# Weight slots at a pitch of 4160 bytes instead of 4096 in a float32 transformer layer

## What is computed

```python
def reference(x, mem, rel_bias, ln_g, ln_b, ffn_w_gate, ffn_w_up, ffn_w_down, w_in, ...):
    for l in range(DEPTH):
        x = layer_norm(ALPHA * x + 0.5 * swiglu(x, ffn_w_gate[l, 0], ffn_w_up[l, 0], ffn_w_down[l, 0]), ...)
        x = layer_norm(ALPHA * x + hybrid_mixer(x, w_in[l], conv_w[l], ...), ...)
        x = layer_norm(ALPHA * x + memory_attention(x, mem, xq_w[l], xkv_w[l], xo_w[l]), ...)
        x = layer_norm(ALPHA * x + 0.5 * swiglu(x, ffn_w_gate[l, 1], ffn_w_up[l, 1], ffn_w_down[l, 1]), ...)
    return x
```

## Time and profile before

| | before |
|---|---|
| median of three runs | 1128.38 us |
| the profiled execution | 1126.32 us |
| its span | 1124.3 us |
| TensorE busy | 1114.1 us (99%) |
| VectorE busy | 776.9 us (69%) |
| ScalarE busy | 531.9 us (47%) |
| mean granted TensorE clock | 0.999 |

### The profile page before, as it was taken

The page is one execution under the profiler, slowest core; times in us unless marked ns, Lnnn a source line. Parts: engine busy times, 40 slices in busy tenths (PEclk is TensorE's granted clock), DMA queues, the critical chain, the costliest instruction groups (busy, mean ns, idle before and its releaser), DMA issues.

```text
span 1124.3 us, 17750 instructions
## 1 busy us (share of the span) xinstructions
PE 1114.1 (99%) x6752; PEld 992.1 (88%) x6752; DVE 776.9 (69%) x1274; ACT 531.9 (47%) x913; POOL 35.5 (3%) x51
## 2 busy tenths in 40 slices
PE   9999999999999999999999999999999999999997
PEld 7899999988888888888898888889899999998886
DVE  4998898753338588774894865557898888863326
ACT  4555555543325477643463453436355555552222
POOL 2000000000002011000000000000000000000000
PEclk9999999999999999999999999999999999999999
DMA  8533333363222222342243242231233333353301
GB/s 286 201 113 113 107 101 111 96 211 94 94 75 89 80 77 84 104 150 75 75 157 126 88 156 75 73 97 58 75 127 99 113 113 96 113 185 99 108 21 75
DMA packets 34121, 123.37 MB, mean 110 GB/s; under 512 B 3916, under 2 KB 3932, under 8 KB 33792
## 3 DMA queue, kind: packets, MB, share of 16 engines
q1 hardware_dynamic: 30528, 109.07, 30.3%
q0 software_dynamic: 3520, 13.29, 3.5%
HBM read 120.23 MB, written 2.11 MB: 109 GB/s over the span
## 4 chain that ended last, share of the span: by engine, by line
PE 94%; DVE 3%; DMA 2%; ACT 1%; issue 0%; DVEq 0%; SPq 0%
PE ps L515 19%; PE ps L516 19%; PE ps L517 19%; PE ps L593 10%; PE ps L594 10%; PE ps L595 10%; DMA raw<-in_units 2%; PE ps L817 1%; PE ps L532 1%; PE ps L796 1%; PE ps L884 1%; PE ps L868 1%; PE ps L789 0%; PE ps L788 0%; PE ps L980 0%
## 5 line engine op out<-in xcount | busy, mean ns | idle before, releaser
L1572 DVE TENSOR_TENSOR wlo<-raw,whi 128x1024 fp32r<-128x1024 f32 x124 | 151.8, 1230 | 171.8 <-ACT whi L1046 170.8
L1046 ACT ACTIVATE whi<-raw 128x1024 fp32r<-128x1024 f32 (+1 forms) x131 | 134.4, 1033 | 135.3 <-PE ps L517 124.2
L515 PE MATMUL ps<-whi,hhi 128*128 128x512 f32 x480 | 187.9, 391 | 0.0
L517 PE MATMUL ps<-whi,hlo 128*128 128x512 f32 x480 | 186.9, 389 | 0.0
L516 PE MATMUL ps<-wlo,hhi 128*128 128x512 f32 x480 | 186.8, 389 | 0.0
L515 PE MATMUL ps<-xth,whi 128*128 128x512 f32 (+1 forms) x340 | 129.6, 381 | 0.0
L517 PE MATMUL ps<-xth,wlo 128*128 128x512 f32 (+1 forms) x340 | 127.5, 375 | 0.0
L516 PE MATMUL ps<-xtl,whi 128*128 128x512 f32 (+1 forms) x340 | 127.4, 375 | 0.0
L517 PEld LDWEIGHTS ps<-whi,hlo 128*128 128x128 f32 x480 | 90.1, 188 | 19.0
L515 PEld LDWEIGHTS ps<-whi,hhi 128*128 128x128 f32 x480 | 90.1, 188 | 18.5 <-ACT km L1046 0.3
L516 PEld LDWEIGHTS ps<-wlo,hhi 128*128 128x128 f32 x480 | 90.2, 188 | 17.9
(11 more groups left out here) (258 smaller groups left out, 2639.1 us busy)
## 6 DMA issues: line engine op xcount, KB each, us to landing
raw<-in_units SPq DMA_DIRECT2D x204, 512.0 KB, 3.5
xraw<-in_units POOLq DMA_DIRECT2D x1, 2048.0 KB, 13.3
xn<-in_x POOLq DMA_DIRECT2D x4, 512.0 KB, 15.2
gb<-in_ln_g POOLq DMA_DIRECT2D x4, 512.0 KB, 3.8
gb<-in_ln_b POOLq DMA_DIRECT2D x4, 512.0 KB, 5.3
wb<-in_bias_by_key POOLq DMA_DIRECT2D x8, 256.0 KB, 3.0
out<-xn SPq DMA_DIRECT2D x8, 256.0 KB, 2.1
gsp<-g_rows POOLq DMA_DIRECT2D x1, 1024.0 KB, 5.1
```

What stands on the lines that cost most here:

```text
L515: mm(dst, lh, rh, start=start, stop=False)
L517: return mm(dst, ll, rh, start=False, stop=stop)
L1046: return nc.scalar.activation(*a, **k)
L1572: v.tensor_tensor(wlo[c % SPL][:, :], raw[c % RAW][:, :], whi[c % SPL][:, :].bitcast(F32), ALU.subtract).then_inc(lo_done, 1)
```

## The change

The six high slots and the six low slots follow each other every 4160 bytes instead of 4096; a slot keeps its 4096 bytes, and 64 are left empty behind it. Another 256 empty bytes follow the low slots, so that all that is allocated after them lies 1024 bytes higher than before. `fast_slot` counts in the new pitch. No instruction is added, removed or reordered.

```diff
+PITCH = 4160
...
         whi_at = cursor[0]
-        whi = [sb(f"whi{s}", [P, D], F32R) for s in range(SPL)]
+        whi = [at(f"whi{s}", [P, D], whi_at + s * PITCH, F32R) for s in range(SPL)]
+        cursor[0] += SPL * PITCH
         wlo_at = cursor[0]
-        wlo = [sb(f"wlo{s}", [P, D], F32R) for s in range(SPL)]
+        wlo = [at(f"wlo{s}", [P, D], wlo_at + s * PITCH, F32R) for s in range(SPL)]
+        cursor[0] += SPL * PITCH + 256
...
         def fast_slot(n, par, j):
 
-            return (U_FFN[n] + 2 * FAST0 + 3 * par + j) % SPL * 4 * KB
+            return (U_FFN[n] + 2 * FAST0 + 3 * par + j) % SPL * PITCH
```

## The result

| | before | after |
|---|---|---|
| median of the runs shown | 1128.37 us | 1132.70 us (1131.25 to 1133.36) |
| ratio, with its 95% interval | | 1.0036 [1.0024, 1.0049] |
| the profiled execution | 1126.32 us | 1132.67 us |
| its span | 1124.3 us | 1130.6 us |
| mean granted TensorE clock | 0.999 | 0.998 |

The kernel is 0.36% slower. 1121.2 was predicted, with a range of 1114.5 to 1130.

What follows compares the result with a forecast made beforehand. TensorE was taken to bound the kernel, its time a count of matmuls times their pitch. Gains of 8.6 and 1.0 us less 2.4 lost gave 7.2 us, so 1121.2 us from 1128.38, range 1114.5 to 1130.

Steps and rivals of the forecast that it cites:

- Fast tiles: First and second feed-forward tiles: 36 of 72 slot matmuls each drop from 120 to 113.3 ns, saving 8.6 us.
- the parity: 256-column matmuls: an odd operand distance in 64-byte lines runs at 113.3 ns, an even one at 120.0.
- `seh` keeps its 448: Fast tiles: the `seh` weights move along with the activations, so their distance stays 448.
- Keys and start of the second feed-forward: Other 256-column matmuls with slot weights: 144 get faster by 6.67 ns each, saving 1.0 us.
- 512-column matmuls: Wide matmuls, 112 units: 2.4 us lost as distance parity changes between units; bounds 4.8 us by resettling, 9.0 us steady.
- Wide matmuls settle: 512-column matmuls return to a 227 ns pitch after a disturbance, so a steady loss was left to a rival.
- The resettling: 512-column matmuls: a disturbance at a unit's start, 43 ns in full, half taken, 21 ns a unit.
- (1): Fast-tile pitch split has another cause than place, so nothing happens: 1128.4 us; chance 0.13.
- (2): Banks repeat over four lines, so only distances of a multiple of 256 collide: 1117.2 us; chance 0.17.
- (3): Only distance 448 is clean, some 544 matmuls gain: 1127.2 us; chance 0.07.
- (4): Odd half of the wide matmuls pays 6.7 ns steadily, 9.0 us against 9.6 gained: 1127.8 us; chance 0.08.
- (5): Wide matmuls clean only at today's distances, 256 and 0; 13.0 us lost against 9.6 gained: 1131.8 us; chance 0.15.

Runs made afterwards that it cites:

- e5: Against the kernel before: only the fast tiles' sums lie 64 bytes off their slots (one 448 early), plain slots keep place 0, gaps added; 1111.53 us.
- e1: Against the kernel before: high slots unmoved, low slots 384 bytes further (place 128), pitch 4096; 1139.79 us.
- e3: Against the kernel before: all slots 192 bytes higher, distance 448 from the activations (place 192); 1136.39 us.
- m128: Against the kernel before: all slots 384 bytes higher, distance 128 from the activations; 1138.81 us.
- m192: Against the kernel before: all slots 448 bytes higher, distance 192 from the activations; 1136.49 us.
- m384: Against the kernel before: all slots 128 bytes higher, distance 384 from the activations (place 128); 1138.93 us.
- e2: Against the kernel before: slots every 4160 bytes, with 128 more bytes between high and low slots so both parts share one place; 1131.97 us.
- m064: Against the kernel before: all slots 320 bytes higher, distance 64 from the activations; 1116.43 us.
- e4: Against the kernel before: all slots 64 bytes higher, distance 320 from the activations (place 64); 1118.54 us.
- m320_by_act: Against the kernel before: slots unmoved, everything behind them 960 bytes higher, so every slot is at distance 320; 1117.24 us.
- e0_shift_only: Against the kernel before: slots unmoved, everything behind them 1024 bytes higher; 1128.25 us.

## Why the prediction was wrong

**What bounds the kernel: right.** In every run the time follows the pitches of TensorE. VectorE's cover was enough even where all of a tile's loss is gone (9.52 us in e5), and its wait there is still 0.75 us, not the 0.53 that were forecast.

**Fast tiles: right in kind, four fifths of the size.** -8.6 us was forecast; the pitch gives 2592 x 2.62 ns = 6.8. Slots 1 and 3 did get fast and slots 0 and 4 stayed slow. The hypothesis behind it, an even or odd number of 64-byte lines, is half right. Only the odd places show 113.3 ns, but both also show 117.7 to 117.8, and at 192 every fast tile runs at that; place 128 costs a little less than place 0 (118.7 against 120.0). The one settled row on which the parity stood, `seh` at 448, shows only one of the two levels of its place. In the kernels whose slots lie at place 0 or 64 it runs at 113.3 ns, in e1, e3, m128, m192 and m384 at 117.7, and in after at 115.5 on average, which costs the 0.9 us that "`seh` keeps its 448" put at nothing. (The aside on attention names the pairs wrongly: the earlier trace rows has `kml` with `qxh` and `kmh` with `qxl`. Their distances, 0 and 64, are right.)

**Keys and start of the second feed-forward:** -0.7 for -1.0.

**512-column matmuls: the step that failed.** The prediction put them at 2.4 us lost and at 9.0 at the most; they lost 6.7 + 3.2 = 9.9. Three things were wrong with it. "Wide matmuls settle" was drawn from a trace in which all of them lie at place 0, the only one at which they run at 226.7 ns. That 227 is twice 113.3 was read as immunity, whereas place 0 is best for wide and worst for narrow matmuls. And the upper bound let only the odd distances pay, though 128 costs 5.7 ns too. The nearest row was there: the gate matmuls at 230 ns, of which I took the excess for a resettling that a unit pays once at the most. After's `down` runs at 230.4. The resettling was sized about right (some 18 ns a unit in e2, against the 21 assumed); what the prediction lacked is the steady price of the place, 2.2 to 6.7 ns on each step.

**The sum from the table.** Two of three matmuls use a unit's high slot, one its low slot. With each slot's two places, `down` should take 228.6, 230.4, 230.5, 231.8, 228.6 and 230.4 ns in slots 0 to 5, on average 230.1 against 226.7; measured are 230.4. For the fast tiles the same working gives 117.5; measured is 117.4. So prices by place come near to after's total. That they add up like this is not shown, though, and the match may be luck in part. e1 has the places 0 and 128 in every unit: its `down` settles to 233.3 where the sum is 228.6, and its wide matmuls lose 13 us in all where the sum is 5.2. That is more than with all slots at 128 (232.4), so there two places taking turns cost something of their own. In after itself slots 0 and 4 have the same two places, and settle to 228.8 and 231.2 ns. How two places taking turns choose their level stays open.

**The rivals.** (1) falls: one place for all slots moves the time by up to 22 us, between m064 and m384. (2) had the period right, 256 bytes, and its clean places wrong. (3) falls: at 448 the fast tiles run at 117.7, at 64 and 320 at 113.3. (4) saw that wide matmuls can pay 6.7 ns steadily, which they do at one odd distance (64: 233.3) and not always at the other (192: 228.9 or 233.3), and it missed 128. (5) is what happened: wide matmuls are clean only at the distances that they have today. Its price was 13.0 us against 9.6 gained; measured are 9.9 against 7.5, less 0.9 on `seh`. Both terms were too large by some 3 us, so that its 1131.8 comes within 1 us of the result is luck in part. The argument that was held against it, that wide matmuls settle within ten steps wherever they repeat, says nothing of the level at which they settle.

**The rule of the Trainium skill** (SBUF — State Buffer, "Who interferes with whom"), that TensorE's two read ports are independent and that it never waits on anyone, gives no reason for the nine kernels of the table to differ. They lie between 1116.4 and 1138.9 us with the same instructions, so for these float32r matmuls the measurement decides against reading it that way. Whether the ports are where the time goes no run shows.

## What to carry to other kernels

Where matmuls stand start to start, look at the pitch of each kind, by operand width and by which operand a buffer is, before moving a buffer: the address that is best for one kind may be the worst for another. A pitch read at a single distance says nothing of other distances, however steady it is, so a price for them has to be bounded by the worst steady excess that any kind shows, on all of the matmuls that move. Once the prices are measured with all buffers at one place, give each kind its own place, and time it, since prices needn't add up where two places take turns (e1); here that is worth 1.55%, where the slots at every 4160 bytes lost 0.36%.

## What the runs showed of the hardware

The pitch of float32r matmuls goes by the distance between the place of the weights and that of the moving operand, modulo 256 bytes: 113.3 to 120.0 ns for 256 columns, 226.7 to 233.3 ns for 512. Moving either operand has the same effect (e4 and m320_by_act). The distance at which the fast tiles' 256 columns are cheapest (64 bytes) is the dearest for 512, and 0 is the other way about. The place alone does not set the pitch: 256 columns run at 113.3 or 117.8 ns at 64 (m064) and at 192 (m192), 512 columns at 228.9 or 233.3 at 192 (e3), in stretches of one kernel. What chooses between the levels no run shows. Whether banks or something else stand behind the distances no run shows. After waits of 1.8 to 2.5 us at the opening of the first fast stage, the profiles of after, e0_shift_only, e3_all_448 and e5_both_best have a stretch at the lower granted clock (0.51 over 3.5 us in after); why that opening is late in some of them was not tried.
